# A two-block kernel: the key norms, the triangular solve and the bonus products of its time-mix stage in another order

## The reference, cut to what matters

```
h = rms_norm_2(x, mix_norm[l])
p = h @ w_in[l]
p_rw, p_pool = p[..., :RWKV_COLS], p[..., RWKV_COLS:]
p_rw = p_rw + (token_shift(p_rw) - p_rw) * mu_shift[l]
p_r, p_k, p_v, p_w, p_a, p_g = jnp.split(p_rw, split_points, axis=-1)
...
def step(state, inp):
    r_t, w_t, k_t, v_t, kk_t, a_t = inp
    sa = jnp.einsum('bhvk,bhk->bhv', state, -kk_t)
    state = (state * w_t[:, :, None, :]
             + sa[..., None] * (kk_t * a_t)[:, :, None, :]
             + v_t[..., None] * k_t[:, :, None, :])
    return state, jnp.einsum('bhvk,bhk->bhv', state, r_t)
...
bonus = jnp.sum(r * k * r_k, axis=-1, keepdims=True) * v
```

## Time and profile before

| | us |
|---|---|
| median of three executions (lowest, highest) | 1572.39 (1572.25, 1577.9) |
| profiled execution, its device time | 1576.84 |
| its span in the profile | 1575.0 |
| PE busy, share of the span | 1488.2, 94% |
| DVE busy | 573.5, 36% |
| ACT busy | 505.9, 32% |
| POOL busy | 762.4, 48% |

### The profile page before, as it was taken

How to read it: one execution, slowest core, us unless ns; L and a number is a source line. 1 busy time by engine, 2 the same in 40 slices (tenths; PEclk the granted TensorE clock), 3 DMA queues, 4 the chain that set the end, 5 groups by cost and what they waited for, 6 DMA issues and landing times.

```text
span 1575.0 us, 20286 instructions
## 1 busy us (share of the span) xinstructions
PE 1488.2 (94%) x7294; PEld 1230.4 (78%) x7294; DVE 573.5 (36%) x798; ACT 505.9 (32%) x694; POOL 762.4 (48%) x1013
## 2 busy tenths in 40 slices
PE   5787999999999999999999999789899999999997
PEld 5675888888888788888888778578867888888887
DVE  6796342222001842222000666844544322221003
ACT  4424343333212432222211673122233332232112
POOL 0362464555555755545555645360045654555553
PEclk9888999999999999999999999889999999999999
DMA  8871244222322223223222222000022422323221
GB/s 316 320 267 41 94 134 147 93 93 96 105 93 93 81 93 107 93 93 103 97 93 93 77 75 68 27 1 1 1 67 82 132 88 98 96 91 107 94 80 54
DMA packets 44545, 156.90 MB, mean 100 GB/s; under 512 B 4944, under 2 KB 7376, under 8 KB 44240
## 3 DMA queue, kind: packets, MB, share of 16 engines
q1 hardware_dynamic: 44496, 156.22, 29.5%
HBM read 154.11 MB, written 2.10 MB: 99 GB/s over the span
## 4 chain that ended last, share of the span: by engine, by line
PE 80%; DVE 13%; ACT 4%; issue 1%; DMA 1%; POOL 0%; SPq 0%; DVEq 0%; ACTq 0%; POOLq 0%
PE ps L1575 24%; PE ps L1577 24%; PE ps L1576 24%; DVE mod_acc L1034 2%; DVE act_lo L1034 1%; DVE tri_x L1031 1%; DVE tri_p L1031 1%; PE ps L1931 1%; DVE xT L1034 1%; DVE act_lo L1031 1%; PE ps L1885 1%; PE ps L1588 1%; ACT w_hi L629 1%; DVE hid_lo L1034 1%; PE ps L1987 1%
## 5 line engine op out<-in xcount | busy, mean ns | idle before, releaser
L464 POOL TENSOR_TENSOR w_lo<-raw,w_hi 128x256 fp32r<-128x256 f32 x932 | 696.1, 780 | 730.6 <-ACT w_hi L629 661.0
L1575 PE MATMUL ps<-act_hi,w_hi 128*128 128x512 f32 x1328 | 529.0, 398 | 15.2 <-DVE act_lo L1031 10.8
L1576 PE MATMUL ps<-act_lo,w_hi 128*128 128x512 f32 x1328 | 520.8, 392 | 0.0
L1577 PE MATMUL ps<-act_hi,w_lo 128*128 128x512 f32 x1328 | 520.4, 392 | 0.0
L629 ACT ACTIVATE w_hi<-raw 128x1024 fp32r<-128x1024 f32 x233 | 244.8, 1054 | 451.0 <-PE ps L1577 423.6
L1575 PEld LDWEIGHTS ps<-act_hi,w_hi 128*128 128x128 f32 x1328 | 251.8, 190 | 78.7 <-issue 13.2
L1576 PEld LDWEIGHTS ps<-act_lo,w_hi 128*128 128x128 f32 x1328 | 251.8, 190 | 53.7 <-issue 2.7
L1577 PEld LDWEIGHTS ps<-act_hi,w_lo 128*128 128x128 f32 x1328 | 251.6, 189 | 53.3
L1575 PE MATMUL ps<-hid_hi,w_hi 128*128 (+3 forms) x584 | 220.2, 377 | 9.8 <-DVE hid_lo L1034 6.3
L1576 PE MATMUL ps<-hid_lo,w_hi 128*128 (+3 forms) x584 | 219.6, 376 | 0.0
L1577 PE MATMUL ps<-hid_hi,w_lo 128*128 (+3 forms) x584 | 219.6, 376 | 0.0
(11 more groups left out here) (265 smaller groups left out, 1149.6 us busy)
## 6 DMA issues: line engine op xcount, KB each, us to landing
raw<-weight_units SPq DMA_DIRECT2D x233, 512.0 KB, 3.3
wm_ring<-mod_units SPq DMA_DIRECT2D x16, 512.0 KB, 6.2
wm_mid<-mod_units SPq DMA_DIRECT2D x16, 512.0 KB, 7.0
wm_early<-mod_units SPq DMA_DIRECT2D x8, 512.0 KB, 9.2
wm_late<-mod_units SPq DMA_DIRECT2D x8, 512.0 KB, 5.5
x_tok<-tokens SPq DMA_DIRECT2D x4, 512.0 KB, 5.0
xT<-tokens_by_channel SPq DMA_DIRECT2D x1, 2048.0 KB, 15.3
result<-act_out SPq DMA_DIRECT2D x16, 128.0 KB, 1.8
```

Of the source, the lines that this page charges most:

```text
L464: ins = nc.gpsimd.tensor_tensor(w_lo[:, slot, c], raw[:, slot, c], w_hi[:, slot, c].bitcast(f32), SUB)
L1575: nc.tensor.matmul(o, wh, xh, start=start, stop=False, **check)
L1576: nc.tensor.matmul(o, wh, xl, start=False, stop=False, **check)
L1577: return nc.tensor.matmul(o, wl, xh, start=False, stop=stop, **check)
```

## The change

Nothing is computed differently. Six things are moved or handed over:

- ACT's `tri_out(0)` copies the diagonal blocks of pairs 0 and 1 first and releases `tri_left`; the blocks for `off` come behind, and `tri_out(1)` comes one unit later. The four diagonal copies of pairs 2 and 3 are taken over by DVE (`tri_right`, at unit 8). DVE's transpose waits for `tri_left`, no longer for all of `tri_out`.
- DVE: `receptance(0)` moves from unit 10 to unit 8, `receptance(1)` from unit 11 to unit 9. The solve begins at unit 9 rather than at unit 10, and one of its steps stands between `normed` and `shifted` of each of the units r1, r2, r3, v2 and v3. `bonus(2)` and `bonus(3)` stand ahead of the last solve steps.
- PE: `key_sums` is split in two, behind unit 5 and behind unit 6. `bonus_product(2)` and `(3)` move from behind unit 15 to behind unit 16.
- ACT: `key_square(2)` and `(3)` stand ahead of `exponentials(2)` and `(3)`.
- DVE: `key_norms` moves from the start of unit 7 to the middle of unit 6.
- POOL: the four products `rK <- rBonus * rK` move from behind the low part of unit 13 to behind that of unit 11.

```
@@ scalar
             def key_norms():
-                after(sem("ss_mm"), 1)
+                after(sem("ss_mm"), 2)
...
+                if pp == 0:
+                    for e in range(4):
+                        r = slice(e * SB, (e + 1) * SB)
+                        ins = nc.scalar.activation(tri_g[r, dst, :].rearrange("q (h n) t -> q h n t", h=2), src[r, :, :, e % 2 * SB:(e % 2 + 1) * SB], ACT.Copy)
+                    ins.then_inc(sem("tri_left"), 1)
+                else:
+                    after(sem("tri_right"), 4)
                 for e in (0, 2):
...
@@ vector
+            def tri_right():
+
+                after(sem("tri_mm"), PAIRS)
+                src = ps[:, 6:8, :].rearrange("q h (n t) -> q h n t", t=CH)
+                for e in range(4):
+                    r = slice(e * SB, (e + 1) * SB)
+                    chain(nc.vector.tensor_copy(tri_g[r, 2 * NSYS:4 * NSYS, :].rearrange("q (h n) t -> q h n t", h=2), src[r, :, :, e % 2 * SB:(e % 2 + 1) * SB]), "tri_right")
...
-                after(sem("tri_read"), PAIRS // 2)
+                after(sem("tri_left"), 1)
                 chain(nc.vector.transpose(tri_m[:, :, :], tri_g[:, :, :].rearrange("p n t -> p t n")))
...
                     normed(name, p)
-                    if i == 11:
-                        receptance(1)
+                    if i >= 9:
+                        solve_steps(1)
...
-                if i == 10:
+                if i == 8:
                     receptance(0)
-                    solve_steps(2)
-                if i == 11:
+                    tri_right()
+                if i == 9:
+                    solve_steps(1)
+                    receptance(1)
+                if i in (10, 11, 14, 15, 16):
                     solve_steps(4)
...
-            solve_steps(SB)
             bonus(2)
             bonus(3)
+            solve_steps(SB)
@@ tensor
+                    key_sums(0)
                 if i == 6:
-                    key_sums()
+                    key_sums(1)
...
-                if i == 15:
+                if i == 16:
                     bonus_product(2)
                     bonus_product(3)
```

More of the change, by code:

```diff
@@ L531, in _ @@
             nc.gpsimd.memset(tri_x[:, :, :].rearrange("p t s -> p (t s)")[:, 0:SB * SB:SB + 1], 1.0).then_inc(sem("tri_unit"), 1)
-            low_through(U_IN + 11, U_IN + 14)
+            low_through(U_IN + 11, U_IN + 12)
             for p in range(PAIRS):
@@ L535, in _ @@
                 nc.gpsimd.tensor_tensor(rK[:, p, :], rBonus[:, p, :], rK[:, p, :], MUL).then_inc(sem("key_in"), 1)
-            low_through(U_IN + 14, U_OUT)
+            low_through(U_IN + 12, U_OUT)
             pool.wait_ge(sem("r_used"), PAIRS)
@@ L822, in tri_out @@
                 dst = slice(pp * 2 * NSYS, (pp + 1) * 2 * NSYS)
+                if pp == 0:
[5 more added lines that the diff above has]
+                    after(sem("tri_right"), 4)
                 for e in (0, 2):
                     r = slice(e * SB, (e + 1) * SB)
[L825 to L828, removed]
+                    ins = nc.scalar.activation(off[r, dst, :].rearrange("q (h n) t -> q h n t", h=2), src[r, :, :, SB:CH], ACT.Copy)
                 ins.then_inc(sem("tri_read"), 1)
@@ L854, in _ @@
                     tri_out(0)
+                if i == 10:
                     tri_out(1)
@@ L872, in _ @@
                     key_gain(3)
+                    key_square(2)
+                    key_square(3)
                     exponentials(2)
                     exponentials(3)
-                    key_square(2)
-                    key_square(3)
             n_step = [0, 0]
@@ L1343, in _ @@
                     decay(3)
-                if i == 7:
-                    key_norms()
                 if i == 8:
@@ L1362, in _ @@
                     key(2)
+                    key_norms()
                     raw_removal(2)
@@ L1785, in gate_product, with key_sums @@
                 nc.tensor.matmul(ps[:, 6 + p % 2, :], g_lora[:, p * P:(p + 1) * P], gx[:, 0, :], start=True, stop=True).then_inc(sem("g_mm"), 1)
-            def key_sums():
+            def key_sums(pp):
                 after(sem("za_read"), PAIRS - 1)
-                for p in range(PAIRS):
+                for p in (2 * pp, 2 * pp + 1):
                     after(sem("sq_ready"), p + 1)
```

8 lines of the change are left out of this document (2 added, 6 removed).

## The result

The change makes the kernel faster. The median goes from 1572.32 us (six executions, 1568.25 to 1577.9) to 1560.22 us (six, 1557.14 to 1564.33); the ratio is 0.992 with a 95% interval of 0.9903 to 0.9937. That is -12.1 us, and the interval reaches from -9.9 to -15.3 us.

The account below looks back on a forecast made before the run. DVE, idle early and then late, was taken to bound PE's start of the pair phase. DVE -2.2, -11.5, +2.9, -1.0; PE's start -11.8, then -0.5: -12.3 us off the median 1572.39, giving 1560.1 us, range 1556.5 to 1567.

Parts of the forecast that it names:

- Term 1: Key sums and unit 7: halves spare a clock fall, so the removals and all behind them on DVE come 2.2 us earlier.
- first rival: Key sums: the clock falls in a half anyway, or did not fall in faster executions before; 1562.3 us, chance 0.26.
- Term 2: DVE's waits between removals and the read of pool3, 12.5 us: receptances, copies and solve steps fill 11.5 us.
- Term 3: Four 32x512 triangle copies added to DVE, 0.69 us each plus gaps: +2.9 us.
- second rival: DVE from unit 9 on stays the bound for longer, by dearer copies or solve-step surcharges; 1566 us, chance 0.11.
- Term 4: Last two solve steps move behind the read of pool3, -1.0 us; POOL's moved products bring nothing, surcharges cancel.
- the sum by the row: DVE solve instructions beside POOL's work: surcharge of 0.42 us from the trace rows, rather than 0.7 by the skill's rule.
- PE's side: Input projection on PE: rkt wait and its clock fall go, PE waits 2.2 us for DVE, pair phase starts 11.8 earlier.
- Term 5: Start of the pair phase: DVE's 4.4 us of moved work is covered; between 0 and 1.4 us won, -0.5 taken.
- the other branch: Start of the pair phase: the clock stays up over PE's short wait, DVE becomes the limit and 1.4 us are won.
- fourth rival: Pair phase: changed hand-overs make PE's clock fall more often, up to 3.4 us each; 1572.4 to 1581 us, chance 0.04.

Follow-up runs that it names:

- norms_only: Kernel before with only key_norms moved to the middle of unit 6; M (gate products behind unit 5 to pair phase's first transposes) 93.77 us.
- joined: Kernel after with key sums in one piece behind unit 6; M 84.26 us against 84.98, PQ (pair phase's first transposes to first pool product) 121.87.
- early_solve: Kernel after with key sums, squares and norms put back where the kernel before has them; M 87.52 us, PQ 124.34.
- best: Kernel after with four bonuses and last two solve steps behind pool3's read, first bonus products behind unit 12, key sums whole; 1559.98 us, ratio 0.9932.
- act_copies: Kernel after with ACT copying all diagonal blocks, none on DVE; M 85.02 us against 84.98.
- split_only: Kernel before with only the key sums split in two halves; M 95.91 us.
- delay: Kernel after with three extra DVE products on a scratch tile ahead of the read of pool3; M 86.54 us against 84.98, M + PQ 208.45.
- no_fill: Kernel after with the five solve steps between a unit's read and its shift moved behind the shift; M 87.63 us, 2.65 longer than after.
- late: Kernel after with the four bonuses and the last two solve steps behind the read of pool3; M 83.54 us, M + PQ 206.84.
- bonus12: Kernel after with the first two bonus products behind unit 12 instead of 13; M 84.45 us, M + PQ 204.79.

## Why the prediction was right, point by point

The forecast was 1560.1 us, the measurement 1560.22; PE's start of the pair phase was to come 11.8 us earlier and came 11.62 earlier, counted from M's start. The sum held, but terms 1, 2, 4 and 5 each had something wrong, and the errors of 2 and 4 cancelled.

**Term 1, the key sums: the amount nearly right, most of the cause wrong.** The removals came 1.85 us earlier against the profiled execution before (29.52 to 27.67) where 2.2 were predicted. Three parts make this up. Without the fall they come 0.98 earlier (28.54 in the second execution of before); `key_norms` at unit 6 brings 1.67 more (26.87 in norms_only), the edit on which I had set a small cost, 0.2; and the split puts 0.81 back (27.67 against 26.86 in joined). The step of the prediction that failed is that the split brings the 2.2 us by sparing the fall. The fall was worth 1.2 us of M, and the split itself costs 0.5 to 0.7.

Whether the split spares the fall stays open. With the sums in one piece the clock fell in three profiled executions (before, early_solve, best) and stayed up in three (the second one of before, norms_only, joined). With the sums in halves it stayed at 1.00 in all eight. So my first rival was right that the fall comes and goes, and wrong that without it nothing is left; but the fall was only ever seen with undivided sums, and fourteen executions are too few to call that a rule. By these numbers, a fall in half of the executions at 1.2 us each, the split would about pay for itself and no more. That is an estimate.

**Term 2, the idle time: right place, 1.4 us too much.** Of 12.5 us of waits 11.5 were to go; 10.1 went. Left are 0.87, 0.15 and a wait that I missed, 1.42 us for the first bonus product. It is new because the receptances come earlier and the products did not. I had looked at who waits for `rkt` and not at whose buffer `rkt` is.

**Term 3, the copies: 0.69 us each, as taken from the earlier trace rows.** Four take 2.85 us with their gaps. By act_copies they cost nothing on the path: without them DVE waits for 2.71 us at the same place, so what term 3 charges for them comes back in term 2. The second rival's rule that each us more on DVE from unit 9 on is a us on the path thus fails in front of unit 9. By its own figures it would have left -7.2 or -8.1 us, and not -6.5.

**Term 4: the surcharges did not cancel, they went down.** DVE's busy time in the stretch is +0.14 us, where +2.85 for the copies and -0.82 for the two solve steps would give +2.0. Most of the difference is cheaper instructions: counted against the fastest of the same shape, 17 have a surcharge above 0.15 us, of 0.39 to 0.47, 7.2 us in all, where before had 21 with 8.7 us.

The largest of the 21 shows something that term 4 had put at nothing, POOL's four products. POOL in the kernel before, and DVE beside it:

```profile
967.88 5.49 POOL L535 TENSOR_TENSOR rK<-rBonus,rK 128x512 f32<-128x512 f32 x4
```

```profile
970.99 1.22 DVE L1031 TENSOR_TENSOR tri_x<-tri_x,tri_p 128x31 f32<-128x31 f32 x1
```

An addition of the same shape takes 0.19 us at 1017.31, so the surcharge is 1.02. The same 1.22 us are there in the second execution of before, in norms_only and in split_only. With its two neighbours (0.11 and 0.21) the products cost DVE 1.3 us in the old place, where it had no waits. In the kernel after they lie beside the removals, which take 0.69 us as before, and this addition takes 0.66 us beside `w_lo`. So up to 1.3 us of the gain may come from moving them. No run moves them alone; what they bring to M is not shown.

The cheaper instructions made good what term 2 lacked, and the stretch shrank by 9.8 us, beside 9.6 predicted (11.5 and 1.0 less 2.9).

The Trainium skill ("SBUF — State Buffer", section "Who interferes with whom") has the later of the two engines blocked until the other's instruction ends, which could be 0.7 us. The trace of the kernel after has 0.42 us for most of the 17 and none of 0.7, so beside `w_lo` the sum by the row was the better one. The 1.02 us above fits the page: if POOL's four products are equally long, the third ends at about 972.0, 1.0 us behind that instruction's start (an estimate from the two rows).

**PE's side: right.** The `rkt` wait and the fall behind it are gone (the granted clock is 1.00 over the whole stretch above, 0.94 in the earlier trace rows), unit 7 takes 5.6 us (931.72 to 937.31), 5.5 predicted, and PE waits for 2.67 us at the end, 2.2 predicted. delay shows that DVE is the one that sets this point.

**Term 5, the pair phase: too small.** I took -0.5. DVE's first product comes 4.37 us after PE's start (1010.32 - 1005.95) and without a wait; before it was 5.83. That is the 1.46 us of the other branch: the clock stayed up over the wait. I let one row decide, the 0.51 behind a wait of 2.92 us in the earlier trace rows. The other branch, that a fall leaves nothing, was wrong too: in joined, no_fill and delay the first transposes ran at half speed (1.11, 1.12 and 1.11 us), and DVE's first product still came 4.77, 4.59 and 4.80 us after PE's start. The half speed ended sooner: over the first 5 us joined was granted 0.67 and before 0.50.

The rest of PQ gained more, 3.8 us in all (3.35 between the second executions). Counted from the start of PQ, the kernel after is 1.46 us ahead at the second transposes (9.18 against 10.64), 3.03 behind the first products of `AA` and `TT` (21.75 against 24.78) and 3.80 at the third transposes (60.64 against 64.44); from there to the end it gains nothing more. At the products of `AA` and `TT`, of the kernel before and of the kernel after:

```profile
1038.00:1042.00 4.00, 3.29 (x17) 3.15 (x17) 0.42 (x1) 1.63 (x4) 3.61 (x6) 0.63 0.01 2
```

```profile
1024.00:1028.00 4.00, 4.00 (x35) 3.95 (x36) 0.79 (x2) 1.19 (x2) 3.69 (x5) 1.00 0.00 0
```

The granted clock over PQ is 0.91 before and 0.96 after; by its shortfall that is 22 us at half speed before (2 x 0.09 x 124.4) and 10 after (2 x 0.04 x 120.6). So the fourth rival had the right mechanism, the clock in the hand-overs of the pair phase, with the other sign: fewer falls, not more. That the change made them fewer is not shown, and why is not settled. For it: the four executions with the old order have a PQ of 124.1 to 124.5, and seven of the eight that begin the pair phase as the kernel after does have 120.3 to 121.9. Against: the eighth, early_solve, has 124.34. At `AA` and `TT` both kinds are found in both orders, 2.05 us in norms_only and split_only and 3.68 in early_solve. late and best have their first transposes at 0.66 us, as after does, and yet fall at `AA` and `TT`.

The Trainium skill ("TensorE: Matmul & The Clock Gate", section "HAM oscillation — how this bites in real kernels") says that only longer gaps throttle. Here the waits at one and the same place don't sort that way, and the measurement decides: behind 2.67 us the transposes stay at full speed, behind 2.77 the first are at half.

**The time.** -11.6 and -3.8 make -15.4 for the profiled pair, and -13.8 for the second pair (M + PQ 219.94 and 206.18). The medians differ by 12.1. The forecast of -12.3 met the medians although it had left out 3 us in the pair phase; the scatter of the executions, 1568 to 1578 before and 1557 to 1564 after, is as large as what I left out, so the agreement to 0.1 us is luck.

## What to carry to other kernels

Look for the engine that is idle and then late, and fill its waits with work that is already possible: here that gave about 9 us of the stage with nearly the same instructions. When a consumer is moved forward, ask of each buffer that it writes who must have read it. Work of a second engine can lie beside instructions that it slows or beside ones that it does not, as POOL's four products did here; compare one instruction's duration at both places before you put such a move at nothing. A fall of the clock seen in one profile may be absent from the next of the same kernel, so it takes several executions of either order to say what an order does to it.

## What the runs showed of the hardware that was not expected

The clock at the start of the pair phase. In bonus12 PE waited for 2.13 us, in early_solve for 3.40, and both started at full speed and fell while working:

```profile
1005.83 0.66 PE L1896 MATMUL ps<-const,rAR 128*128 128x128 f32 x4 [2.13 <-DVE pooled L1036]
1006.32 0.62 PE L1896 MATMUL ps<-const,rB 128*128 128x128 f32 x4
1006.75 1.04 PE L1896 MATMUL ps<-const,rK 128*128 128x128 f32 x4
```

```profile
1007.64 0.66 PE L1897 MATMUL ps<-const,rAR 128*128 128x128 f32 x4 [3.40 <-DVE pooled L1036]
...
1008.57 0.74 PE L1897 MATMUL ps<-const,rK 128*128 128x128 f32 x4
1009.11 1.06 PE L1897 MATMUL ps<-const,rV 128*128 128x128 f32 x4
```

Four transposes go from 0.60 to 1.04 and 1.06 us about 1 us behind the wait's end in the one, 1.5 us in the other. In the kernel after, with 2.67 us, they don't. Behind the waits of 4.21 us and more (delay, no_fill and the four executions with the old order) the clock was down at once each time. Below that, the length of the wait alone does not tell whether or when the fall comes, and the duration of the first instruction behind it does not either. In the key sums the clock fell with no wait at all ahead: PE is busy for the full 2.00 us in the windows of early_solve and best above.

Over the whole of PQ the mean granted clock orders the kernels only roughly. PQ is 120.3 to 121.2 us in those with 0.96 and 124.4 and 124.5 in the two executions of before with 0.91, but at 0.93 it is 121.65 in no_fill and 124.34 in early_solve. What a fall costs hangs on where it lies. In norms_only, split_only, early_solve and late one lies at the third transposes; here norms_only, then the kernel after:

```profile
1079.27 1.06 PE L1884 MATMUL ps<-const,rAR 128*128 128x128 f32 x4
```

```profile
1066.59 0.60 PE L1896 MATMUL ps<-const,rAR 128*128 128x128 f32 x4
```

From the third transposes to the fourth these four take 29.5 to 29.7 us, all other executions 28.1 to 28.2. The spread of 4 us in PQ is more than most of the edits tried here bring.
